# One flow-matching layer: x, state and gating transfers moved, the last row group's chain spread over three pairs, and ScalarE scaling every fourth piece of h

## The reference

```python
shift1, scale1, gate1, shift2, scale2, gate2 = jnp.split(mod, 6, axis=-1)   # mod = silu(c) @ w_ada + b_ada
h = rms_norm(x, norm_g_l[0]) * (1 + scale1) + shift1
y, C_out, n_out, m_out = parallel_mixer(h, ...)    # z = h @ w_in; Fourier, pooling and mLSTM branches;
                                                   # (g_f*y_f + g_p*y_p + g_m*y_m) @ w_out, gates from z
x = x + gate1 * rms_norm(y, norm_g_l[1])
h = rms_norm(x, norm_g_l[2]) * (1 + scale2) + shift2
a, b = jnp.split(h @ w_ffn_in_l, 2, axis=-1)
x = x + gate2 * rms_norm((jax.nn.silu(a) * b) @ w_ffn_out_l, norm_g_l[3])
```

## Time and profile before

| | us |
|---|---|
| median of 3 runs (1739.48 to 1744.54) | 1740.62 |
| the profiled execution | 1741.52 |
| its span, first to last instruction | 1739.7 |
| TensorE busy | 1692.2 |
| VectorE busy | 992.7 |
| ScalarE busy | 628.8 |
| GpSimd busy | 222.5 |

### The profile page before, as it was taken

The page is one execution under the profiler, slowest core; times in us unless marked ns, Lnnn a source line. Parts: engine busy times, 40 slices in busy tenths (PEclk is TensorE's granted clock), DMA queues, the critical chain, the costliest instruction groups (busy, mean ns, idle before and its releaser), DMA issues. The chain is left out here.

```text
span 1739.7 us, 24679 instructions
## 1 busy us (share of the span) xinstructions
PE 1692.2 (97%) x9558; PEld 1601.8 (92%) x9558; DVE 992.7 (57%) x1674; ACT 628.8 (36%) x1102; POOL 222.5 (13%) x340
## 2 busy tenths in 40 slices
PE   6899999999999999999999899999999999999996
PEld 3799999989999999998988799999999999888885
DVE  5654443343444444456978886555555553589885
ACT  6311212242322222234667563222222222454452
POOL 1400001322222233311000000000000000000000
PEclk9999999999999999999999999999999999999998
DMA  9655445664455556679876322221122226567683
GB/s 349 234 176 186 163 150 198 227 201 140 165 173 172 186 190 206 198 253 274 265 234 192 141 101 81 76 67 70 60 75 76 76 76 193 152 198 240 187 277 124
DMA packets 155579, 295.74 MB, mean 170 GB/s; under 512 B 12761, under 2 KB 91932, under 8 KB 155466
## 3 DMA queue, kind: packets, MB, share of 16 engines
q1 hardware_dynamic: 111600, 162.69, 28.8%
q0 software_dynamic: 27536, 91.31, 16.0%
q10 hardware_dynamic: 16336, 40.29, 6.3%
HBM read 226.46 MB, written 67.82 MB: 169 GB/s over the span
## 5 line engine op out<-in xcount | busy, mean ns | idle before, releaser
L669 PE MATMUL bank<-h_hi,w_hi 128*128 128x384 f32 x1080 | 370.8, 343 | 7.5 <-DVE h_lo L2658 3.6
L671 PE MATMUL bank<-h_hi,w_lo 128*128 128x384 f32 x1080 | 362.0, 335 | 0.0
L670 PE MATMUL bank<-h_lo,w_hi 128*128 128x384 f32 x1080 | 361.7, 335 | 0.0
L1972 DVE TENSOR_TENSOR w_lo<-raw,w_hi 128x1024 fp32r<-128x1024 f32 x154 | 187.3, 1220 | 143.9 <-ACT w_hi L1482 143.8
L669 PEld LDWEIGHTS bank<-h_hi,w_hi 128*128 128x128 f32 x1080 | 203.4, 188 | 12.3 <-DVE h_lo L2658 5.8
L670 PEld LDWEIGHTS bank<-h_lo,w_hi 128*128 128x128 f32 x1080 | 203.6, 188 | 0.1
L671 PEld LDWEIGHTS bank<-h_hi,w_lo 128*128 128x128 f32 x1080 | 203.1, 188 | 0.0
L1482 ACT CAST w_hi<-raw 128x1024 fp32r<-128x1024 f32 x154 | 159.3, 1052 | 98.8 <-PE bank L671 43.2
L670 PE MATMUL bank<-w_lo,a_hi 128*128 128x512 f32 x352 | 136.9, 389 | 0.0
L671 PE MATMUL bank<-w_hi,a_lo 128*128 128x512 f32 x352 | 136.9, 389 | 0.0
L669 PE MATMUL bank<-w_hi,a_hi 128*128 128x512 f32 x352 | 136.9, 389 | 0.0
(11 more groups left out here) (358 smaller groups left out, 3375.7 us busy)
## 6 DMA issues: line engine op xcount, KB each, us to landing
raw<-in_w_stream SPq DMA_DIRECT2D x144, 512.0 KB, 4.5
z_scratch<-z_st ACTq DMA_DIRECT2D x44, 576.0 KB, 2.9
raw<-in_w_stream SPq DMA_DIRECT2D x90, 256.0 KB, 4.5
raw<-in_w_ada SPq DMA_DIRECT2D x35, 512.0 KB, 4.4
mg<-z_scratch ACTq DMA_DIRECT2D x24, 576.0 KB, 5.3
a_raw<-f_scratch SPq DMA_DIRECT2D x44, 256.0 KB, 3.8
a_raw<-f_scratch SPq DMA_DIRECT2D x22, 320.0 KB, 3.6
zt<-z_scratch POOLq DMA_DIRECT2D x27, 256.0 KB, 4.2
```

The lines of the kernel that those rows point to most:

```text
L669: pe.matmul(out, a_hi, b_hi, start=start, stop=False)
L670: pe.matmul(out, a_hi, b_lo, start=False, stop=False)
L671: return pe.matmul(out, a_lo, b_hi, start=False, stop=stop)
L1972: dve.tensor_tensor(w_lo[:, slot], raw[:, slot], w_hi[:, slot].bitcast(F32), ALU.subtract).then_inc(s_wlo, 1)
```

## The change

- **x stores.** The nine stores of x_in to xp_dram move from GpSimd's queue, after h, to SyncE's, into `z1_turn(0)`: behind the load of w_stream unit 1, which keeps its place, and ahead of the third w_ada load.
- **h.** ScalarE scales k = 2 and k = 6 of each group (one of four), by an activation with scale and bias, ahead of its four casts; VectorE is left with k = 0 and 4, GpSimd keeps the odd k.
- **State.** The two stores of new_C move from before mx_load(2) to the end of e2(0).
- **Gating.** mg_load(0) and (1) move behind the gate evacuations of parts 3 and 4.
- **x_add.** x_add(3g + 1) moves from e1(g + 1) to the end of e2(g).
- **Last e2.** The split of the first ffn unit moves ahead of combine(0), and s_low(0) ahead of t_low(4).
- **Last row chain.** x_add, x_square, x_rstd and x_norm of m = 6, 7, 8 move from pair 0 to the ends of pairs 0 and 1 and the starts of pairs 1 and 2; the stores of x1 tiles 6 to 8 stand behind those of f of pairs 0 and 1.

```diff
--- before.py
+++ after.py
@@ -429,7 +429,7 @@
         s_const, s_rows, s_vec, s_vecc, s_cpad = (sem(n) for n in ("const_landed", "rows_landed", "vec_transposed",
-                                                                   "vec_ready", "c_padded"))
+                                                                   "vec_ready", "c_padded_or_h_full_act"))
         s_set = sem("memsets_done")
@@ -663,7 +663,13 @@
             n = k // KH * pairs * (NG + 1) + (pairs * g + k % KH // 2 + 1 if g < NG - 1 else pairs * g + 2 * (k % KH // 2 + 1))
-            eng.wait_ge(s_hfp if k % 2 else s_hf, n)
+            m = k // KH * (NG + 1) + (g + 1 if g < NG - 1 else g + 2)
+            if k % 2:
+                eng.wait_ge(s_hfp, n)
+            elif k % KH:
+                eng.wait_ge(s_cpad, 1 + m)
+            else:
+                eng.wait_ge(s_hf, m)
 
@@ -783,14 +789,17 @@
 
+            def x_stores():
+                sp.wait_ge(s_padd, 2 * (LAT // P))
+                for c in range(NT):
+                    sp.wait_ge(s_xin[c], 16)
+                    sp.dma_start(xp_dram[c], x_in[:, c]).then_inc(s_xps, 16)
+
             def z1_turn(i, first):
...
                     n0 = ADA_FIRST + 3 * u
-                    if not (first and u == 0):
-                        if first and u == 1:
-                            sp.wait_ge(s_unit, n0 - RAW + 1)
-                        else:
-                            sp.wait_ge(s_arow, i * 32 + ada_done(u - 2, 1))
+                    if not (first and u < 2):
+                        sp.wait_ge(s_arow, i * 32 + ada_done(u - 2, 1))
                         load(n0 % RAW, w_stream[bass.ds(i * RAW + u, 1)])
@@ -803,6 +812,10 @@
                     load((n0 + 2) % RAW, w_ada[bass.ds(i * (2 * RAW) + (ADA_FIRST + 2 * u + 1), 1)])
+                    if first and u == 0:
+                        sp.wait_ge(s_unit, n0 + 3 - RAW + 1)
+                        load((n0 + 3) % RAW, w_stream[1:2])
+                        x_stores()
 
@@ -1516,9 +1529,19 @@
                 act.wait_ge(s_prow, LAT // P)
+                act.wait_ge(s_xn, 2 * NT)
                 for half in range(2):
+                    if half:
+                        act.wait_ge(s_mod, 1)
+                    else:
+                        act.wait_ge(s_modc, 2)
                     for g in range(NG):
                         r = slice(g * GW, (g + 1) * GW)
+                        k = KH * half + 2
+                        for a, b, col in halves(g):
+                            x = xn[:, k, g * GW + a:g * GW + b]
+                            act.activation(x, x, ACT.Identity, bias=mod[:, k, col:col + 1],
+                                           scale=A1[:, k, col:col + 1]).then_inc(s_cpad, 1)
                         for k in range(KH * half, KH * half + KH):
@@ -1653,8 +1676,8 @@
                             act.wait_ge(s_zst[d], 8 * (Z_COUNT - 5))
-                        mg_load(0)
-                        mg_load(1)
+                    if part in (3, 4):
+                        mg_load(part - 3)
                     for k in MX_PARTS[part]:
@@ -1849,10 +1872,10 @@
                         split(n, n)
-                    if j == 0:
-                        x_square(6)
+                    if j == 1:
                         x_norm(6)
                     elif j == 2:
+                        x_norm(8)
                         h2_out(6)
@@ -1864,19 +1887,18 @@
                     act.activation(s1b[:, par], s1b[:, par], ACT.Silu).then_inc(s_pact, 1)
-                    if j == 0:
+                    if j == 1:
                         x_square(7)
...
                         s_high(j + 1)
-                    if j == 0:
+                    if j == 1:
                         x_norm(7)
...
                     act.activation(v1[:, :], v1[:, :], ACT.Silu).then_inc(s_pact, 1)
-                    if j == 0:
-                        x_square(8)
-                        x_norm(8)
+                    if j < 2:
+                        x_square(6 + 2 * j)
                     if j >= LATE:
@@ -2315,9 +2337,7 @@
                     split(n + AHEAD, n + AHEAD)
-                    if g and c == 0:
-                        x_add(m + 1)
-                    elif g and c == 1:
+                    if g and c == 1:
                         x_rstd(m)
@@ -2364,7 +2384,7 @@
                         y_scale(3 * g + 1)
-                    if g < NG - 1 or k not in (3, 4):
+                    if g < NG - 1 or k not in (3, 4, 5):
                         split(n + AHEAD, n + AHEAD)
@@ -2372,6 +2392,7 @@
                             x_add(3 * g)
+                            x_add(3 * g + 1)
                     elif k < 2:
@@ -2384,10 +2405,11 @@
                             t_low(i)
+                        split(n + 2 + AHEAD, n + 2 + AHEAD)
                         combine(0)
                     elif k == 5:
+                        s_low(0)
                         t_low(4)
-                        s_low(0)
 
@@ -2440,27 +2462,27 @@
                         y_scale(8)
-                        x_add(6)
                     dve.wait_ge(s_pact, scalar_step(j, "s1"))
...
                     add("c11", s1b[:, par], s1b[:, par], 2)
+                    if j == 1:
+                        x_rstd(6)
+                        x_add(7)
+                    elif j == 2:
+                        x_rstd(8)
                     if j:
...
                         combine(j + 1)
-                    if j == 0:
-                        x_rstd(6)
-                        x_add(7)
                     if j:
...
                     add("u3", u2[:, :], u2[:, :], 7)
-                    if j == 0:
-                        x_add(8)
+                    if j == 1:
                         x_rstd(7)
@@ -2470,8 +2492,8 @@
                     add("c12", v1[:, :], v1[:, :], 3)
-                    if j == 0:
-                        x_rstd(8)
+                    if j < 2:
+                        x_add(6 + 2 * j)
                     add("c21", u2[:, :], u2[:, :], 4, "u3")
@@ -2647,7 +2669,7 @@
                         dve.wait_ge(s_mod, 1)
-                    if i < len(order) and order[i][1] % 2 == 0:
+                    if i < len(order) and order[i][1] % KH == 0:
                         h_full(dve, order[i][0], order[i][1], s_hf)
@@ -2687,9 +2709,6 @@
             pool.wait_ge(s_padd, 2 * (LAT // P))
-            pool.wait_ge(s_xr, NT)
-            for c in range(NT):
-                pool.dma_start(xp_dram[c], x_in[:, c]).then_inc(s_xps, 16)
             pool.wait_ge(s_xps, 16 * NT)
@@ -2838,8 +2857,6 @@
             hm_load(8)
-            for d in range(2):
-                pool.dma_start(new_C[0, 0, d].rearrange("h k v -> k h v"), st_ctx[:, d, :, 0:DH]).then_inc(s_new, 16)
             mx_load(2)
@@ -2895,6 +2912,7 @@
                     for d in range(2):
+                        pool.dma_start(new_C[0, 0, d].rearrange("h k v -> k h v"), st_ctx[:, d, :, 0:DH]).then_inc(s_new, 16)
                         pool.dma_start(new_n[0, 0, d].rearrange("h k -> k h"), st_ctx[:, d, :, DH], allow_slow_non_contiguous=True).then_inc(s_new, 16)
@@ -2903,11 +2921,13 @@
                 for j in range(PAIRS):
-                    if j == 0:
-                        for m in range(6, 9):
-                            x1_store(m)
                     f_store(0, j, c21[:, :], s_pv, vector_step(j, "f1"))
                     f_store(1, j, v2[:, :], s_pv, vector_step(j, "f2"))
+                    if j == 0:
+                        x1_store(6)
+                    elif j == 1:
+                        x1_store(7)
+                        x1_store(8)
                     if j >= LATE:
...
                 pool.wait_ge(s_prod, product_done(PAIRS - 1, 4))
```

## The result

The changed kernel takes 1725.52 us, the median of 4 runs (1721.56 to 1727.32), against 1741.07 of 4 runs of the kernel before (1739.48 to 1744.54): a ratio of 0.9905, 95% interval 0.9882 to 0.9928. The forecast was 1725.0.

What follows compares the result with a forecast made beforehand. TensorE, busy 97% of the span, was taken as the bound, so only its waits count. Terms 4.7 + 2.0 + 4.4 - 1.7 + 6.9 - 0.7 = 15.6 us gave a median of 1725.0, range 1719.5 to 1733.

Steps and rivals of the forecast that it cites:

- The x stores: TensorE's 3.04 us gap at w_stream unit 2 closes, with 1.7 us of slow clock behind it: 4.7 us gained.
- Rival 4: x stores hold SyncE's queue so the w_ada loads are late instead: 4.7 us back, 1729.7; chance 0.05.
- h: In h GpSimd's pieces get faster where no VectorE scaling stands against them: 2.0 us gained, between 0 and 3.7.
- Rival 1: GpSimd stays as slow in h, held up by the subtractions: the 2.0 us are lost, 1727.0; chance 0.16.
- State and gating: Without new_C ahead of mx_load(2) the 2.70 us mx_lo wait goes, with 1.7 us of clock: 4.4 us gained.
- Rival 3: mx pieces stay late because the gate loads meet the last two: 4.4 us back, 1729.4; chance 0.05.
- x_add(3g + 1): Same VectorE work in another order before the gated sums: 0, within 0.5 us either way.
- Last e2: Gaps of 1.27 and 0.95 us become one of 2.2 to 2.5 that drops the clock: 1.7 us lost.
- The last row chain: TensorE's 4.14 us gap in the last row chain closes, with 2.8 us of slow clock: 6.9 us gained.
- The 0.7 for short waits in pairs 1 to 3: Moved chain fills ScalarE in pairs 1 and 2, h2_out(6) waits for the last x1 store: 0.7 us lost.
- Rival 2: The chain stalls pair 1 or 2 as it did pair 0, ScalarE full: 6.9 us back, 1731.9; chance 0.11.
- rival 5: The chain stalls each of pairs 1, 2 and 3, 8 us a pair: 1749, slower than before; chance 0.03.

Runs made afterwards that it cites:

- experiment 9: Changed kernel with GpSimd's scaling of the odd k in h left out, so not a valid layer: 1719.33 us in one execution.
- experiment 6: Changed kernel with the old h, VectorE scaling k = 2 and 6 again: 1726.58 us, ratio 0.9920.
- experiment 8: experiment 7 plus ScalarE also scaling k = 3 and 7 of the third token group in h, instead of GpSimd: 1723.94 us, ratio 0.9906.
- experiment 3: Kernel before with new_C moved into e2(0) and the two mg loads behind parts 3 and 4, nothing else: 1733.90 us, ratio 0.9962.
- experiment 10: Kernel before with only the two new_C stores moved into e2(0): 1735.80 us, ratio 0.9975.
- experiment 11: Kernel before with only the two mg loads moved behind parts 3 and 4: 1739.88 us, ratio 0.9999.
- experiment 7: Changed kernel with t_low(3) and t_low(4) behind y_scale(6) and y_scale(7) in the last e2: 1726.98 us, ratio 0.9920.
- experiment 4: Kernel before with only the last row group's chain spread over the pairs, and its x1 stores: 1734.31 us, ratio 0.9965.
- experiment 2: Kernel before with only ScalarE's scaling of k = 2 and 6 in h: 1739.43 us, ratio 1.000.
- experiment 5: Changed kernel with the order of the last e2 put back: 1725.67 us, ratio 0.9911.
- experiment 12: experiment 8 plus the x1 stores of tiles 7 and 8 ahead of pair 1's f stores on GpSimd's queue: 1721.99 us, ratio 0.9892.

## Why the prediction was right, and where it was not

**The x stores: right.** 4.7 us forecast, 4.8 in the profile, 4.8 alone by paired matmuls and 5.9 by the times. The 1.7 of it for the clock was taken over from the gap of 2.70 us; behind its own gap the kernel before lost 1.5. The load of unit 2 is issued at 64.83 and cast at 68.54, 3.7 us later where it took 8.7; the nine stores are issued from 41.01 in 7.9 us. From SyncE's queue of the changed kernel:

```profile
41.01 7.92 SPq L796 DMA_DIRECT2D xp_scratch<-x_in  x9
49.03 13.48 SPq L765 DMA_DIRECT2D raw<-in_w_ada  x2
64.83 0.33 SPq L765 DMA_DIRECT2D raw<-in_w_stream  x1
```

Rival 4 fell: no w_ada load holds ada_pair.

**h: the step that failed.** The forecast let GpSimd come down from 1.57 towards 1.07 us wherever no scaling of VectorE stands against it, and took 2.0 us. Measured: 0.24. Rival 1 happened, at 1.8 us where it named 2.0. Two things were wrong. First, the 1.07 was no time of GpSimd alone: that row runs from 39.53 to 40.60, and beside it stood both of VectorE's first scalings,

```profile
39.37 0.87 DVE L660 TENSOR_SCALAR xn<-xn,A,mod 128x384 f32<-128x384 f32 x2
```

And it is not VectorE's scalings alone that hold GpSimd up. In the changed kernel the first two pieces on GpSimd, and VectorE's work beside the second, are

```profile
38.19 0.84 POOL L660 TENSOR_SCALAR xn<-xn,A,mod 128x384 f32<-128x384 f32 x1 [35.76 <-DVE A L2017]
```

```profile
39.02 2.10 POOL L660 TENSOR_SCALAR xn<-xn,A,mod 128x384 f32<-128x384 f32 x1
```

```profile
39.06 1.23 DVE L1994 TENSOR_TENSOR w_lo<-raw,w_hi 128x1024 fp32r<-128x1024 f32 x1 [0.56 <-ACT w_hi L1495]
40.20 1.33 DVE L2680 TENSOR_TENSOR h_lo<-xn,h_hi 128x384 fp32r<-128x384 f32 x2
```

From 39.06 to 41.12 VectorE only subtracts, and GpSimd's piece takes 2.10 us where the one before it took 0.84. So subtractions alone hold GpSimd up. The piece lasts as long as the first and the whole subtraction of w_lo, 0.84 + 1.23 = 2.07; but two subtractions for h_lo fall in it as well, so how much each of them cost it is not shown. The Trainium skill has a rule for this in "SBUF — State Buffer", section "Who interferes with whom": a VectorE operation with two inputs in SBUF contends with a GpSimd one that reads SBUF, and the lock on the port pair that they share is exclusive. The rows agree that they contend. That one waits for the other's end they don't bear out in the other direction: the subtractions that took 547 ns with the old h take 651 on average with the new one, seven of the 24 about 0.85 us, which is 0.3 longer, beside GpSimd rows of over 1 us; with GpSimd idle they take 550 (experiment 9). From the old h (experiment 6) to the new one VectorE's scalings went from 9.0 to 3.8 us in total and its subtractions from 13.1 to 15.6; its idle time up to the end of h went from 0.2 to 1.7, and h_lo ended 0.5 us sooner. So about half of what the scalings gave free went into longer subtractions, and most of the rest into waiting. Second, the forecast asked which engine would get faster, not which one is last: GpSimd works from 38.19 to 57.29 without a break, and ScalarE's split of unit 1 can only follow its last piece:

```profile
57.32 0.51 ACT L1547 CAST h_hi<-xn 128x384 fp32r<-128x384 f32 x1 [1.02 <-POOL xn L660]
57.74 1.04 ACT L1495 CAST w_hi<-raw 128x1024 fp32r<-128x1024 f32 x1
```

With w_lo behind that, TensorE waits 0.82 us at 60.09. Work had to be taken from GpSimd (experiment 8), not from VectorE.

**State and gating: right.** 4.4 forecast, 4.8 in the profile, 4.1 and 4.5 by paired matmuls in experiments 3 and 10 (6.6 and 4.4 by the times). The shorter tail that comes with the move of new_C was in no term. The forecast named new_C as the cause, and 3 and 11 confirm it. Rival 3 is not quite dead: waits of 1.17 and 0.74 us for mx_lo came back in experiments 7 and 8 with the moved transfers, so the pieces have little margin.

**x_add(3g + 1): right**, 0; the gated-sum waits went from 3.1 to 2.9 us.

**Last e2: half right.** One gap was forecast at 2.2 to 2.5 us and is 2.59; but the loss of 1.7 us of clock didn't come. The windows behind the gap, of the changed kernel:

```profile
965.00:967.00 2.00, 2.00 (x11) 1.00 0.00 0
967.00:969.00 2.00, 2.00 (x14) 1.00 0.30 51
```

The step that failed was "its length is nearer to 2.70, which dropped the clock": between 1.8 and 2.7 us the length doesn't tell (below).

**The last row chain: right.** 6.9 forecast, 7.15 in the profile less 0.3 later; in experiment 4 7.1 less 0.3 by paired matmuls, 6.1 (3.7 to 8.5) by the times. The 0.7 for short waits in pairs 1 to 3 was too much: 0.3 in all, nearly all of it at x_turn(7). But the reading behind it held: h2_out(6) does wait 1.0 us for the last x1 store, and ends at 1005.7, where x_turn(7) starts at 1005.81. Rival 2 had almost no margin against it, and any lead that TensorE gains before pair 2 turns into a wait there (experiment 7). Of rival 5 nothing was seen.

**The sum** came out right in part by luck, because two mistakes cancelled: h gave 1.8 us less, and the merged gap cost 1.7 less than forecast. 4.8 + 0.2 + 4.8 + 0 + 6.9 = 16.7 against 15.6, with the tail left out; the difference between the medians is 15.6 too, but with an uncertainty of 4 us either way that agreement says nothing of the terms.

## What to carry to other kernels

When work is moved off an engine, first find the engine that has no idle time up to the stage's last instruction; only what that one sheds is gained, and GpSimd's time beside a VectorE that subtracts from SBUF is made in part by VectorE. A gap of the bound engine is worth something only if the engines behind its next waits are ahead too: with VectorE working without a break, or ScalarE no sooner at the next dependency, closing it moves the wait. For a late transfer look at what was issued just ahead of it, on its own queue (new_C) or on another (the x stores on GpSimd's, the load on SyncE's): moving 2 stores of new_C and 9 of x was worth more than 9 us here, and moving the two mg loads nothing.

## What was not expected of the hardware

Whether a wait of TensorE is followed by the low level of its clock, 1.2 GHz, isn't told by the wait's length between 1.8 and 2.7 us. The loss is counted here as the matmul distances over 0.25 us in the 8 us behind the wait, less 0.173 us each. In the fourteen profiled executions, from 55 us on:

| idle us | followed by | loss us |
|---|---|---|
| 0.7 to 1.28, some 60 times | never a drop | 0.1 to 0.2 (once 1.2 by other, slower shapes at granted clock 1.00) |
| 1.62 | no drop | 0.2 |
| 1.82, 1.94, 2.26, 2.42, 2.70 | drop | 1.3, 1.5, 3.1, 1.7, 1.4 |
| 1.95, 2.58, 2.58, 2.59 | no drop | 0.1 |
| 3.02 to 3.15, 6 times | drop | 1.5 to 2.8 |
| 4.13 to 4.15, 6 times | drop | 1.5 to 2.8 |

The closest pair is the same wait at x_turn(7), 1.94 us in experiment 7 and 1.95 in experiment 8. Windows behind it, in that order:

```profile
1009.40:1011.40 2.00, 1.97 (x11) 0.67 0.71 166
1011.40:1013.40 2.00, 2.00 (x8) 0.50 0.88 356
```

```profile
1005.90:1007.90 2.00, 2.00 (x15) 1.00 0.75 158
1007.90:1009.90 2.00, 2.00 (x13) 1.00 0.91 365
```

The granted clock is 0.67 and 0.50 in the first and 1.00 in the second. And one gap, the same to 0.02 us in six executions (4.13 to 4.15), cost between 1.5 and 2.8 us of slow matmuls. A forecast can only put a chance on such a loss. What decides it was not tried. The place may matter as well as the length: all four waits of 1.82 to 2.70 us for mx_lo in e1 were followed by a drop, none of the three of 2.58 and 2.59 ahead of product 6 was, and x_turn(7) had it once in two.

Nor does a drop need a wait. In four of the executions (experiments 2, 5, 11 and 12) the clock fell between 396 and 404 us with no wait of TensorE over 0.15 us in the 12 us before; what stands there, in every kernel, is a row of 18 small matmuls (16x16) in 2.18 us. Each time it cost about 1.5 us. The row and the windows in experiment 12, and last a window behind the same row in the changed kernel, where the clock stayed:

```profile
392.39 2.18 PE L1158 MATMUL bank<-base,gz 16*128 16x16 f32 x18
```

```profile
394.00:396.00 2.00, 2.00 (x14) 0.98 0.79 244
396.00:398.00 2.00, 2.00 (x8) 0.50 0.00 0
```

```profile
396.00:398.00 2.00, 2.00 (x14) 1.00 0.03 7
```
